# Shares of the weight split between VectorE and GpSimd, and the places of twelve side steps, in a two-block fp32 transformer kernel

## The reference, cut to what matters

```python
u = rms_norm(h, norm_mix_pre)                       # first block
q, kc, vc, ks, vs, kw, vw, g, q_s, k_s, v_s, ga, gb = split(u @ w_in)
kc = gelu(blocks(kc + pos_k) @ w1_k) @ w2_k         # compressed keys; values alike
o_a = nsa_attention(q, kc, vc, ks, vs, kw, vw, g, bias)
o_b = swa_sink_attention(q_s, k_s, v_s, sinks, bias)
h = h + rms_norm((sigmoid(ga) * (o_a @ w_up_nsa) + sigmoid(gb) * (o_b @ w_up_swa)) @ w_out)
h = h + rms_norm(relu(rms_norm(h) @ w_mlp_in) ** 2 @ w_mlp_out)

xn = rmsnorm(h, mix_norm_w)                         # second block
xa, qkv, z, beta_logit, a_logit, gate_a, gate_b = split(xn @ w_in_2)
y_a = pool_mixer(xa) @ w_pool_up
g = -exp(a_log) * softplus(a_logit + dt_bias); beta = sigmoid(beta_logit)
gc = cumsum(g, in chunks of 64)                     # decay = exp(gc_i - gc_j)
y_b = (rmsnorm(gated_delta_rule(silu(conv(qkv)), g, beta)) * silu(z)) @ w_dn_up
h = h + (sigmoid(gate_a) * y_a + sigmoid(gate_b) * y_b) @ w_mix_out
q = rmsnorm(h, ffn_norm_w) @ w_query                # expert layer
v1, i1 = top_k(q1 @ keys_1, 16); v2, i2 = top_k(q2 @ keys_2, 16)
top, pos = top_k(v1 + v2, 16); experts = (i1 * 128 + i2)[pos]
h = h + sum(softmax(top) * gelu(x . down[experts]) * up[experts])
out = rmsnorm(h, final_norm_w)
```

## Time and profile before

| | |
|---|---|
| median of 3 runs | 1532.38 us (1532.05 to 1533.7) |
| the profiled execution | 1532.05 us, span 1530.3 us |
| PE busy | 1503.2 us, 98% of the span |
| PEld busy | 1421.5 us, 93% |
| DVE busy | 1031.5 us, 67% |
| ACT busy | 841.2 us, 55% |
| POOL busy | 343.9 us, 22% |
| DMA | 255.15 MB, mean 167 GB/s |
| granted TensorE clock, mean | 0.997 of full speed |

### The profile page before, as it was taken

How to read it: one execution, slowest core, us unless ns; L and a number is a source line. 1 busy time by engine, 2 the same in 40 slices (tenths; PEclk the granted TensorE clock), 3 DMA queues, 4 the chain that set the end, 5 groups by cost and what they waited for, 6 DMA issues and landing times.

```text
span 1530.3 us, 29210 instructions
## 1 busy us (share of the span) xinstructions
PE 1503.2 (98%) x11442; PEld 1421.5 (93%) x11442; DVE 1031.5 (67%) x1816; ACT 841.2 (55%) x1648; POOL 343.9 (22%) x382
## 2 busy tenths in 40 slices
PE   7999999999989999999999999999999999999998
PEld 7888999999989999999999999999999888888887
DVE  5666665555688764688999957777774555555554
ACT  4576464444565544554444557777775554444444
POOL 1242430000337553402566610011112000000000
PEclk9999999999999999999999999999999999999999
DMA  7952555555445632465455554444445666666664
GB/s 209 255 159 89 174 177 184 183 180 184 134 126 164 184 97 85 137 192 171 159 179 181 171 180 142 144 141 138 139 139 180 194 195 194 194 195 193 195 193 138
DMA packets 76805, 255.15 MB, mean 167 GB/s; under 512 B 9359, under 2 KB 15325, under 8 KB 76541
## 3 DMA queue, kind: packets, MB, share of 16 engines
q1 hardware_dynamic: 76429, 252.63, 52.9%
q0 software_dynamic: 240, 0.66, 0.2%
HBM read 250.23 MB, written 2.75 MB: 165 GB/s over the span
## 4 chain that ended last, share of the span: by engine, by line
PE 84%; DVE 11%; ACT 2%; issue 1%; SPq 1%; DMA 1%; POOL 1%; POOLq 0%; DVEq 0%; ACTq 0%
PE bank L682 83%; DVE wl L1699 3%; DVE big L1699 2%; DVE big L2262 1%; DVE big L2273 1%; ACT wh L1264 1%; DVE big L2269 1%; DVE big L1702 1%; ACT big L1264 1%; DMA raw<-in_wst 1%; DVE big L2258 1%; DVE big L2279 1%; DVE big L2266 1%; PE bank L1013 0%; POOL big L2421 0%
## 5 line engine op out<-in xcount | busy, mean ns | idle before, releaser
L1699 DVE TENSOR_TENSOR wl<-raw,wh 128x1024 fp32r<-128x1024 f32 (+4 forms) x467 | 543.8, 1165 | 375.2 <-ACT wh L1264 374.8
L1264 ACT ACTIVATE wh<-raw 128x1024 fp32r<-128x1024 f32 (+1 forms) x467 | 489.9, 1053 | 317.5 <-PE bank L682 308.7
L682 PE MATMUL bank<-gw,wh 128*128 128x256 f32 x3504 | 648.6, 286 | 2.1 <-ACT wh L1264 2.1
L682 PEld LDWEIGHTS bank<-gw,wh 128*128 128x128 f32 x3504 | 545.9, 192 | 2.5 <-issue 2.2
L682 PE MATMUL bank<-gw,wl 128*128 128x256 f32 x1752 | 496.6, 283 | 2.4 <-POOL wl L2421 2.3
L682 PEld LDWEIGHTS bank<-gw,wl 128*128 128x128 f32 x1752 | 336.0, 192 | 3.3 <-issue 1.8
L682 PE MATMUL bank<-xw,wh 128*128 128x256 f32 x1696 | 321.3, 290 | 9.5 <-ACT wh L1264 7.6
L682 PE MATMUL bank<-wh,xw 128*128 128x512 f32 x1056 | 325.3, 389 | 0.0
L682 PEld LDWEIGHTS bank<-xw,wh 128*128 128x128 f32 x1696 | 266.8, 193 | 17.0 <-ACT wh L1264 7.9
L1264 ACT ACTIVATE big<-bank 128x256 f32<-128x256 f32 (+23 forms) x327 | 118.1, 372 | 244.8 <-PE bank L682 208.0
L682 PE MATMUL bank<-xw,wl 128*128 128x256 f32 x848 | 241.5, 285 | 0.0
(11 more groups left out here) (141 smaller groups left out, 1109.7 us busy)
## 6 DMA issues: line engine op xcount, KB each, us to landing
raw<-in_wst SPq DMA_DIRECT2D x455, 512.0 KB, 3.5
big<-toeplitz SPq DMA_DIRECT2D x16, 128.0 KB, 6.0
raw<-in_w1k SPq DMA_DIRECT2D x4, 512.0 KB, 6.8
raw<-in_w1v SPq DMA_DIRECT2D x4, 512.0 KB, 4.5
big<-in_xT SPq DMA_DIRECT2D x4, 256.0 KB, 5.3
raw<-in_wst SPq DMA_DIRECT2D x4, 256.0 KB, 4.7
diag_in<-big SPq DMA_DIRECT2D x2, 512.0 KB, 3.3
big<-in_keys SPq DMA_DIRECT2D x1, 1024.0 KB, 5.4
```

Of the source, the lines that this page charges most:

```text
L682: return e.matmul(o, a, b, start=first, stop=last, skip_group_check=True)
L1264: return e.activation(o, x, f, **kw)
L1699: return e.tensor_tensor(o, a, b, f)
```

## The change

It changes the shares of the split in seven stretches of units and moves a dozen side steps by a tick or more on PE, ACT, DVE and POOL. No arithmetic is added or removed.

```diff
 def lo_share(u):
-    if 16 <= u < UPA + 6:
+    if TM + 2 <= u < UPA + 6:
         return 448
...
     if u in (MLP + 2, XA + 2):
-        return 512
-    if CK <= u < CK + 6 or CQVZ + 18 <= u < DU + 2:
+        return 896
+    if PGA + 1 <= u < CK + 2:
+        return 512 if u < CK else 384
+    if CK + 2 <= u < CK + 6 or CQVZ + 18 <= u < DU + 2:
         return 384
-    if QU + 5 <= u < DN + 2:
+    if QU + 2 <= u < DN + 2:
         return 320
...
-        ACC_POOL = (0, 1, 3)
+        ACC_POOL = (0, 1, 3, 4)
...
-        SUMS_AT = {(2, 0): 0, (XA + 2, 1): 4, (QU + 2, 0): 5}
+        SUMS_AT = {(2, 0): 0, (XA + 2, 0): 4, (QU + 2, 0): 5}
... (PE, gates)
-                    yield from clock.until(XA + 3, 0)
+                    yield from clock.until(XA + 3, 1)
                     e.wait_ge(*gaA.at("bat"))
...
-                    yield from clock.until(PGA + 1, 1)
+                    yield from clock.until(PGA + 2, 0)
                     e.wait_ge(*gaD.at("ga"))
... (ACT, compress_side)
-                    yield from clock.until(11, 0)
+                    yield from clock.until(10, 3)
... (ACT, gates_side)
-                    yield from clock.until(XA + 2, 3)
+                    yield from clock.until(XA + 3, 0)
                     e.wait_ge(*baP.at("ba"))
...
-                    yield from clock.until(PGA + 1, 2)
+                    yield from clock.until(PGA + 2, 1)
                     e.wait_ge(*baP.at("cum"))
... (DVE, turn)
-                    if n == 3:
-                        for c in range(8):
-                            add_square(4, c)
... (DVE, gates_side)
-                    yield from clock.until(XA + 3, 0)
+                    yield from clock.until(XA + 3, 1)
                     e.wait_ge(*baP.at("tr"))
...
+                    yield from clock.until(PGA, 0)
                     e.wait_ge(*gaA.at("small"))
...
-                    yield from clock.until(PGA + 1, 3)
+                    yield from clock.until(PGA + 2, 3)
                     e.wait_ge(*gaA.at("egc"))
... (DVE, main loop)
-                    if u == 2:
-                        mean(0)
-                    if u in (XA + 2, QU + 2):
-                        split(u + 2)
-                        mean(4 if u < QU else 5)
-                    if u != XA + 3:
-                        split(due(u))
+                    if u == XA + 2:
+                        split(XA + 4)
+                    if (u, 0) in SUMS_AT and u < QU:
+                        mean(SUMS_AT[u, 0])
+                    split(due(u))
                     for q in range(4):
+                        if q == 0 and u == QU + 2:
+                            mean(5)
                         if (u, q) in SPREAD_AT:
                             catch_up(s)
                         clock.tick()
-                        if q == 0:
-                            split(due(u))
... (POOL, turn)
+                    if n == 3:
+                        for c in range(8):
+                            add_square(4, c)
... (POOL, topk_side)
-                            yield from clock.until(QU + 5 + (t + 1) // 4 + n, (t + 1) % 4)
+                            yield
                             x = flat(room).rearrange("p (t k i) -> p t k i", t=2, i=16)
                             e.wait_ge(*tkD.at((h, "eq", n)))
```

## The result

The change takes 1545.05 us (median of 4 runs, 1544.48 to 1547.18) against 1533.04 (4 runs, 1532.05 to 1533.74): a ratio of 1.0084, interval 1.0072 to 1.0096. It is slower, by 12 to 13 us; 1540.3 was forecast, and the time lies inside the range. The span of the profiled execution grew from 1530.3 to 1543.6. (The new shares stand in five stretches of units, 10 to 15, 59, 123, 126 to 129 and 195 to 197, not in seven.)

A forecast was written before the change was run, and what follows sets the result against it. PE, busy 98% of the span, was taken as the bound, so any new wait is paid in full. Terms 2.8 + 0.5 + 1.6 + 2.6 + 0 + 0.7 + 0 = +8.2 on 1532.05 gave 1540.3 us, range 1532.3 to 1546.5.

The forecast's parts named there:

- likeliest case: Whole kernel: the band of 1537 to 1543.5 us around the forecast of 1540.3.
- the top-k or another slow stretch: Rivals where top-k losses add up or another slow clock stretch comes; chance 0.15 together with the decays' wait.
- The price of the shares: POOL and two-input DVE subtractions exclude each other: a half cut at 512 takes 1.95 us instead of 1.23.
- Units 10 to 15: Shares and gw copies ahead of unit 13's high half delay DVE's biases, for which PE's scores wait: +2.8 us.
- turn(1): Unit 59: POOL's 896 columns run 0.75 us longer ahead of DVE's first add to H: +0.5, from 0 to +0.8.
- turn(3): Unit 123: +0.5 for the 896 columns, and PE's earlier sums wait 1.1 us for square-adds on POOL: +1.6.
- Units 126 to 137: Chain to unit 131: four halves of 512 on POOL cost DVE 0.7 each, less 0.2: +2.6 us.
- The decays' wait: PE waits about 4 us at the decays' transpositions, less at unit 131: counted 0; uncovered, a rival at 1544.3 us.
- QU+2: Norm 5's power on POOL ends later behind three halves of 320, so PE's spread waits: +0.7 us.
- Top-k: Low halves come 1.27 us later once per head, but PE takes it back at the end: 0, -0.3 to +1.3.
- the top-k adds up: Rival: DVE's masks wait on POOL's products, up to 5 of 8 heads: +6.3, 1546.6 us; within a shared 0.15.
- The clock: Half-rate stretch behind the wait at unit 131: 1.7 us could go or come once more; counted 0.

The follow-up runs named there:

- share_and_order: Kernel before with 448 columns of units 10 to 15 on POOL and gw copies ahead of unit 13's high half: 1536.33 us against 1533.54.
- qu_only: Kernel before with 320 columns of units 195 to 197 on POOL and mean(5) behind the third low half: 1534.24 us against 1534.38.
- whole_halves: Kernel before with units 130 and 131 whole on DVE instead of 384 columns on POOL: 1533.37 us against 1533.54.
- pool512_only: Kernel before with 512 columns of units 126 to 129 on POOL, nothing else: 1535.23 us against 1533.90.
- gates_later_only: Kernel before with PE's cumulative sum, ACT's three steps behind it and DVE's product beta*exp three ticks later: 1533.62 us against 1534.38.
- adds_on_pool_only: Kernel before with norm 4's three square-adds on POOL and the sums one tick earlier on PE: 1535.48 us against 1534.38.
- decays_behind: Kernel before with units 130 and 131 whole on DVE and ACT's 16 decay exponentials behind unit 131's high half: 1530.62 us against 1533.54.

## Why the prediction was right, and where it was not

The direction was right, and for the reason given: one pair of engines excludes each other, POOL's new shares gave DVE nothing in the stretches where PE waits, and PE at 98% pays for most new waits. Read where the forecast reads them, in the rows, its five terms above 0 come to 2.9 + 0.6 + 1.7 + 2.6 + 0.8 = 8.6 against 8.2. The value, 1540.3, is 4.75 below the measured time, because the top-k cost 3.84 where I had 0. The time lies above my likeliest case (up to 1543.5) and in one that I gave 0.15, the top-k or another slow stretch; that it is still inside the range, by 1.5 us, owes as much to the range's width as to the sum.

- **The price of the shares.** It held: 0.48 became 1.5 behind a pair of 512, the adds took 3.13 instead of 2.28. The rule of the Trainium skill ("SBUF — State Buffer", "Who interferes with whom") agrees with these numbers too. The Trainium skill's remark that moving work between the two might not help ("Perfetto Trace Analysis", "Optimizing Scalar/DVE Operations") is true of units 126 to 129 and not of the top-k, where taking POOL's share away cost 6.4 us.
- **Units 10 to 15.** 2.8 forecast, and DVE's chain from the adds to the biases was 2.94 longer: this step was right. PE's scores came 2.25 later behind unit 11's end (unit 11 itself was 0.96 late, the adds only 0.28), and the stretch 3.75 longer, because the half-rate piece behind the wait took 1.5 more. That piece I had not counted; share_and_order shows it again.
- **turn(1).** 0.5 forecast, 1.25 measured: 0.6 is the add that POOL's 896 columns hold up, the other 0.66 a half-rate piece at 218.4. share_and_order, which leaves the turn alone, has such a piece at 214.9 at no cost, and qu_only one at 209.7 that cost 0.5.
- **turn(3).** 1.6 against 1.74, and both terms held: 0.6 for the held-up add (0.5 forecast) and 1.08 for the third square-add (1.1 forecast). The half-rate piece at 402 of before isn't there in the change, and that makes no difference: whole_halves hasn't got it either and takes the same 26.49, with 2.46 of idle time instead of 1.85.
- **Units 126 to 137.** The chain to unit 131 was 2.6 longer, as forecast; 2.1 of that is the four pairs (pool512_only), 0.1 the later steps (gates_later_only), and the remaining 0.4 shows only with all edits together. A pair cost 0.5 and not the 0.7 that I had: with DVE first 1.0 less 0.55, and with POOL first (two of the four) DVE's half took 1.75 and 1.78 instead of 1.23. The decays' wait came as forecast, at 443.85 after 3.62 us, and took the place of unit 131's, but to the full: with 0.85 more at the cumulative sum and 1.7 for a half-rate piece at 443.7, PE came to unit 131 6.2 us later than before, where I had room for 5.9. Its high half, ready since 455.0, no longer held PE, which began on it at 456.5; POOL's low half ended at 456.75 and PE's first matmul with it ran at 456.90. So PE's own path and DVE's chain met there within 0.2 us. PE began that low half 2.7 later in the stretch than before; that the whole stretch is only 1.69 longer comes from the half-rate piece that stood behind it before (1.5) and is gone. The wait of 0.62 at the cumulative sum didn't go, it became 1.47 at 437.63, since DVE's series was itself held up.
- **QU+2.** 0.7 against 0.77.
- **Top-k: this step failed.** I wrote "DVE has no gap there and ends the top-k when it did". The first half was nearly true (busy 97%) and contradicts the second: an engine without a gap adds up every hold-up. I had looked at the late half on PE, which the ids' wait indeed takes back by 1.24, and not at what the new order does to DVE: 0.6 us more for each of the seven heads in the stretch, 4.1 in sum. The rival "the top-k adds up" had the right course and the wrong reason and size (6.3).
- **The clock.** I had both ends at 1.7 and the value at 0. The change has three half-rate pieces (at 61.4, 218.4 and 443.7) and before two (at 402.1 and 446.5), outside the program's start and end; their places and lengths differ from kernel to kernel and explain most of the single edits' scatter in the later stretches. A lower mean is not always paid for: in eight of the fifteen executions of the change on record the mean clock was 0.992 against 0.996 in the profiled one, and their times (1544.3 to 1547.9) are no longer than the others'.

What stays open: why the chain to unit 131 is 0.4 longer with all edits than with the single ones added up, what made the stretch between units 138 and 195 0.56 shorter, and what decides whether a wait of 1 to 3 us is followed by a half-rate piece. Most stretches rest on one profiled execution of each kernel.

## What to carry to other kernels

Before work is moved between DVE and POOL, look at what stands next to it on DVE: behind a pair of two-input operations the sum of both durations counts; beside an operation fed from PSUM (0.42 us at 445.49 before) POOL's part cost nothing. One input from SBUF is no safeguard by itself. A TENSOR_SCALAR of 48 columns, 0.19 us before, took 1.14 in the change, where POOL was subtracting from 55.74 on:

```profile
56.24 1.14 DVE L1793 TENSOR_SCALAR big<-big 128x48 f32<-128x48 f32 x1
```

On an engine with almost no idle time hold-ups are kept to the end, even where the engine that waits for it gets its own loss back, so price a reordering on the saturated engine and not on its consumer. And where the bound engine waits for one instruction, ask first what stands ahead of it in its own queue: putting 16 exponentials behind the high half of unit 131, together with two whole halves that alone gave 0.56, made the stretch 3.05 shorter, the only gain in the twelve kernels that is clear of the scatter.

## What the runs showed of the hardware that was not expected

The granted clock falls to 0.50 in stretches of 3.4 or 6.8 us, often shortly behind a wait of PE: at 61.4 behind 1.89 us (the change), at 446.5 behind 2.07 (before), at 416.1 behind 1.36 (adds_on_pool_only). Other waits had none behind them: 1.08 at 419.61 in the change, 2.67 at 435.50 in gates_later_only, 1.06 at 447.86 in decays_behind. Behind one and the same wait of 2.07 or 2.08 at unit 131 the low stretch was 3.4 us long in some kernels and 6.8 in others, and units 126 to 137 took 46.0 to 46.4 with the one and 47.3 to 47.5 with the other.

Such a stretch costs up to half its length, as much as the wait, or nothing where PE would have waited anyway (turn(3), with and without it 26.49). A kernel's small differences (under 0.2%) can be such a piece alone: in gates_later_only the clock's mean over units 126 to 137 was 1.00 instead of 0.96, and the stretch 0.9 us shorter with 0.5 us more idle time on PE.
